# Expert block behind a router: token-major logits, positions ahead of the plan, scatter behind the second projection, last pass written out

## The reference, cut to what matters

```
h = h + concat(y_ssd, y_sc) @ w_out           # y_sc, y_ssd normed in groups
u2 = rmsnorm(h, norm_ffn)
p_group = softmax(u2 @ wg_r + bg_r); g_val, g_idx = top_k(p_group, 1)
sel = (u2 @ we_r + be_r) of the chosen group;  top_v, top_i = top_k(sel, 2)
combine = one_hot(g_idx) * g_val * softmax(top_v) at top_i
for e in 16 experts (4 groups of 4):
    out += combine[:, e] * ((silu(u2 @ w_gate[e]) * (u2 @ w_up[e])) @ w_down[e])
return rmsnorm(h + out, norm_final)
```

## Time and profile before

| | us |
|---|---|
| median of 3 runs (lowest, highest) | 1699.01 (1698.69, 1701.52) |
| the profiled execution's own time | 1698.8 |
| its span in the trace | 1697.0 |
| TensorE busy in the span | 1619.1 (95%) |
| end of the output projection, about | 1350.7 |
| first expert matmul | 1375.25 |
| last matmul of the last D3 ends | 1682.67 |

### The profile page before, as it was taken

One profiled execution on the slowest core, in us unless ns is written; L12 is line 12 of the kernel. 1 busy time (PEld: TensorE's weight loads), 2 busy tenths in 40 slices (PEclk: granted clock), 3 DMA queues, 4 the chain that ended last, 5 costly groups with the idle time before them and its releaser, 6 DMA issues.

```text
span 1697.0 us, 30496 instructions
## 1 busy us (share of the span) xinstructions
PE 1619.1 (95%) x11968; PEld 1502.0 (89%) x11968; DVE 1143.2 (67%) x1392; ACT 872.9 (51%) x1044; POOL 120.8 (7%) x89
## 2 busy tenths in 40 slices
PE   6999999989999999999998999999999879999996
PEld 6999978879999999997887999989999768778785
DVE  6655666656555655567666555578687479888887
ACT  5434434554433643443465443385535256767775
POOL 1000051010000100014001000021210000000000
PEclk9999999999999999999999999999999989999998
DMA  7766641145565566664013655646432759898993
GB/s 237 241 193 195 155 149 51 42 124 183 176 195 176 173 215 200 186 169 142 29 51 125 199 187 183 180 127 196 149 111 96 265 160 366 303 359 307 350 311 120
DMA packets 238218, 313.02 MB, mean 184 GB/s; under 512 B 51172, under 2 KB 176676, under 8 KB 238132
## 3 DMA queue, kind: packets, MB, share of 16 engines
q1 hardware_dynamic: 237520, 310.75, 56.6%
q10 hardware_dynamic: 612, 1.14, 0.2%
HBM read 310.82 MB, written 1.05 MB: 184 GB/s over the span
## 4 chain that ended last, share of the span: by engine, by line
issue 49%; PE 38%; DVE 3%; POOLq 3%; POOL 2%; ACT 2%; DVEq 1%; DMA 1%; SPq 0%; ACTq 0%
PE psum L416 6%; PE psum L418 6%; PE psum L417 6%; PE psum L2653 3%; PE psum L2652 3%; PE psum L2654 3%; PE psum L2675 2%; PE psum L2676 2%; PE psum L2677 2%; PE psum L2611 1%; POOL TMP L427 1%; POOLq L433 1%; POOLq L1518 1%; POOL QCOS L1533 1%; PE psum L2633 1%
## 5 line engine op out<-in xcount | busy, mean ns | idle before, releaser
L408 DVE TENSOR_TENSOR unit_low<-unit_raw,unit_high 128x2048 fp32r<-128x2048 f32 (+1 forms) x186 | 429.6, 2310 | 224.2 <-ACT unit_high L402 224.1
L416 PE MATMUL psum<-UH,unit_high 128*128 128x256 f32 x1888 | 541.8, 287 | 17.1 <-DVE UL L466 13.8
L417 PE MATMUL psum<-UL,unit_high 128*128 128x256 f32 x1888 | 534.8, 283 | 0.0
L418 PE MATMUL psum<-UH,unit_low 128*128 128x256 f32 x1888 | 534.5, 283 | 0.0
L402 ACT ACTIVATE unit_high<-unit_raw 128x2048 fp32r<-128x2048 f32 (+1 forms) x186 | 347.8, 1871 | 120.2 <-PE psum L418 119.7
L416 PEld LDWEIGHTS psum<-UH,unit_high 128*128 128x128 f32 x1888 | 361.1, 191 | 22.6 <-DVE UL L466 16.1
L417 PEld LDWEIGHTS psum<-UL,unit_high 128*128 128x128 f32 x1888 | 360.0, 191 | 1.6 <-issue 1.4
L418 PEld LDWEIGHTS psum<-UH,unit_low 128*128 128x128 f32 x1888 | 361.3, 191 | 0.0
L2395 DVE TENSOR_TENSOR unit_low<-unit_raw,unit_high 128x2048 fp32r<-128x2048 f32 x99 | 222.3, 2286 | 29.3 <-ACT unit_high L2391 29.3
L2391 ACT ACTIVATE unit_high<-unit_raw 128x2048 fp32r<-128x2048 f32 x99 | 184.7, 1917 | 14.8 <-PE psum L2677 8.7
L417 PE MATMUL psum<-HL,unit_high 128*128 128x256 f32 x640 | 178.9, 280 | 0.0
(11 more groups left out here) (490 smaller groups left out, 2503.1 us busy)
## 6 DMA issues: line engine op xcount, KB each, us to landing
unit_raw<-in_ffn_wg SPq DMA_DIRECT2D x44, 1024.0 KB
unit_raw<-in_ffn_wu SPq DMA_DIRECT2D x44, 1024.0 KB
unit_raw<-in_ffn_wd SPq DMA_DIRECT2D x44, 1024.0 KB
unit_raw<-in_w_in SPq DMA_DIRECT2D x36, 1024.0 KB
unit_raw<-in_expert_w_gate SPq DMA_DIRECT2D x34, 1024.0 KB, 7.4
unit_raw<-in_expert_w_up SPq DMA_DIRECT2D x33, 1024.0 KB, 7.8
unit_raw<-in_expert_w_down SPq DMA_DIRECT2D x32, 1024.0 KB, 7.3
unit_raw<-in_w_out SPq DMA_DIRECT2D x10, 1024.0 KB
```

What stands on the lines that cost most here:

```text
L408: dve.tensor_tensor(low[s][:, 0:w], raw[s][:, 0:w], high[s][:, 0:w].bitcast(F32), ALU.subtract).then_inc(unit_low, 1)
L416: pe.matmul(dst, wh, xh, start=start, stop=False, skip_group_check=True)
L417: pe.matmul(dst, wh, xl, start=False, stop=False, skip_group_check=True)
L418: return pe.matmul(dst, wl, xh, start=False, stop=stop, skip_group_check=True)
```

## The change

Two edits lie in the hybrid part. TensorE's `states(1)` waits for `yd1`, one VectorE instruction earlier than `yt1`. The short norm's last piece gets a tile of its own (`H`), its deviation is made before the SSD branch's, and its norm and split stand ahead of units 3 and 4 on VectorE. The logits are made with X held still, two products of 20 columns for each k, directly token-major, and half of the transposes and logits stand inside the projection's last unit, before its last two output tiles.

In the router, ScalarE and VectorE take expert unit 0 ahead of the logits, one of four squares goes to VectorE as `tensor_tensor_reduce`, half of `UTF` goes to GpSimd, positions and `select` stand ahead of the plan. Five units are split ahead instead of three. In a pass the scatter stands behind U0, T3 ahead of the gather; a projection waits for that half of `UL` which it reads. The last pass is written out behind the loop: no gather, no units ahead, T3 between the two units of D2, h's last split in `UH` and `UL`. The split of y, the scatter and the tail's sums and outputs go by halves of 512 columns.

The core of the diff (8 columns of indentation are taken off):

```diff
         elif h == 15:
-            pe.wait_ge(EM.sem, EM.at("yt1"))
+            pe.wait_ge(EM.sem, EM.at("yd1"))
...
+        for n in range(2):
+            mm = pe.matmul(psum[:, 0, n * 20:n * 20 + 20], X[:, k, META + n * P:META + n * P + P], WRG[:, k, :],
+                           start=(k == 0 and n == 0), stop=(k == KT - 1), skip_group_check=True)
         if k == KT - 1:
...
             if u == 7 and d % 2 and d < KT - 1:
                 mm.then_inc(QM.sem, QM.inc(f"out{d // 2}"))
+            if u == 7 and d == 5:
+                for n in range(4):
+                    to_tokens(n)
...
-    for k in range(KT):
-        to_tokens(k)
+    for n in range(4, KT):
+        to_tokens(n)
...
+def short_dev(j):
+    return (H if j == 3 else SG)[:, :, 0:T]
...
+        if kind == 2 and j in (1, 2):
             short_high(j - 1)
+    short_std(3)
     y_std(2)
+    short_high(2)
     w_high(act, 3)
-    short_std(3)
     w_high(act, 4)
     short_high(3)
...
         dve.wait_ge(BM.sem, BM.at(f"sc_std{j}"))
-        dve.reciprocal(SG[:, :, 0:T], SG[:, :, 0:T])
...
     def short_low(j):
...
             for gq in range(4):
                 pair_weights(2, gq)
-        elif i == 11:
-            short_low(2)
     normed_outputs(2)
+    short_low(2)
+    short_norm(3)
     w_low(dve, 3)
-    short_norm(3)
+    short_low(3)
     w_low(dve, 4)
-    short_low(3)
     w_low(dve, 5)
...
     w_low(dve, 7)
+    expert_low(dve, G2, 0)
...
-AHEAD = 3
+AHEAD = 5
...
+def last_h(j, more):
+    return (hh4, hl4) if more or j < 3 else (UH[:, 0:4, 0:P], UL[:, 0:4, 0:P])
...
-    pe.wait_ge(BM.sem, BM.at("xt1"))
-    gather_pe(pe, 0)
+    pe.wait_ge(EM.sem, EM.at("position"))
...
 def router_act(act):
+    expert_high(act, 0, G2, 0, used(G2, EU - 2))
     act.wait_ge(QM.sem, QM.at("x_t0"))
     for n in range(2):
         ins = act.activation(XTK[:, n, 0:512], psum[:, 4 + 2 * n, :], ACT.Copy)
     ins.then_inc(BM.sem, BM.inc("xt0"))
     for n in range(2):
         act.activation((sg_flat, h_flat)[n], psum[:, 4 + 2 * n, :], ACT.Square, accum_out=SS[:, n, 0:1])
-    expert_high(act, 0, G2, 0, used(G2, EU - 2))
+    expert_high(act, 0, G2, 1, used(G2, EU - 1))
...
+       .then_inc(BM.sem, BM.inc("ss"))
     act.wait_ge(EM.sem, EM.at("ss_sum"))
     act.activation(RS[:, 2:4], RS[:, 0:2], ACT.Sqrt, scale=1.0 / D, bias=eps[:, :]).then_inc(BM.sem, BM.inc("u_std"))
-    for n in range(2):
-        ins = act.activation(XTK[:, n, 512:D], psum[:, 5 + 2 * n, :], ACT.Copy)
-    ins.then_inc(BM.sem, BM.inc("xt1"))
-    expert_high(act, 0, G2, 1, used(G2, EU - 1))
+    act.activation(XTK[:, 0, 512:D], psum[:, 5, :], ACT.Copy).then_inc(BM.sem, BM.inc("xt1"))
     act.wait_ge(EM.sem, EM.at("g_sub"))
...
+    expert_high(act, 0, G2, 2)
     evacuate_act(act, 0)
-    expert_high(act, 0, G2, 2)
+    expert_high(act, 0, G2, 3)
+    expert_high(act, 0, G2, 4)
     act.wait_ge(EM.sem, EM.at("t_sub"))
     act.activation(RT[:, :, 84:85], RT[:, :, 84:85], ACT.Exp).then_inc(BM.sem, BM.inc("t_exp"))
...
+    dve.tensor_copy(XTK[:, 1, 512:D], psum[:, 7, :])
+    dve.drain()
+    dve.tensor_tensor_reduce(out=hl4.rearrange("p m s -> p (m s)"), in0=XTK[:, 1, 512:D], in1=XTK[:, 1, 512:D], scale=1.0, scalar=0.0,
+                             op0=ALU.mult, op1=ALU.add, accum_out=SS[:, 1, 1:2])
+    dve.drain()
     dve.wait_ge(BM.sem, BM.at("ss"))
     dve.tensor_tensor(RS[:, 0:2], SS[:, :, 0], SS[:, :, 1], ALU.add).then_inc(EM.sem, EM.inc("ss_sum"))
     dve.drain()
     dve.wait_ge(BM.sem, BM.at("u_std"))
     dve.reciprocal(RS[:, 0:2], RS[:, 2:4])
...
-    dve.wait_ge(BM.sem, BM.at("xt1"))
-    for n in range(2):
-        dve.tensor_tensor(UTF[:, n, 512:D], XTK[:, n, 512:D], GAINF[:, 512:D], ALU.mult)
+    four = "p n (g e) -> p n g e"
+    dve.tensor_tensor(c(40, 56).rearrange(four, g=4), c(4, 20).rearrange(four, g=4),
+                      c(32, 36).unsqueeze(3).to_broadcast([P, 2, 4, 4]), ALU.mult)
+    dve.drain()
+    dve.tensor_reduce(c(102), c(108, 112), AX, ALU.add)
+    dve.tensor_reduce(c(56, 60), c(40, 56).rearrange("p n (g e) -> p n e g", g=4), AX, ALU.add)
+    dve.drain()
+    dve.tensor_scalar(c(103), c(102), -1.0, float((GROUPS - 1) * P), ALU.mult, ALU.add)
     dve.wait_ge(QM.sem, QM.at("counts"))
     dve.tensor_tensor(c(104, 108), psum[:, 2, 0:8].rearrange("p (n f) -> p n f", n=2), c(32, 36), ALU.mult)
+    dve.drain()
+    dve.tensor_reduce(c(100), c(104, 108), AX, ALU.add)
+    dve.drain()
+    dve.scalar_tensor_tensor(out=c(101), in0=c(100), scalar=float(P), in1=c(103), op0=ALU.is_gt, op1=ALU.mult)
+    dve.scalar_tensor_tensor(out=c(104), in0=c(100), scalar=-1.0, in1=c(102), op0=ALU.add, op1=ALU.add)
+    dve.drain()
+    dve.tensor_tensor(POSQ[:, :], RT[:, :, 101], RT[:, :, 104], ALU.add)
+    dve.tensor_tensor(POS0[:, :], RT[:, :, 101], RT[:, :, 104], ALU.add).then_inc(EM.sem, EM.inc("position"))
+    select(dve)
...
-    select(dve)
     expert_low(dve, G2, 1)
-    evacuate_dve(dve, 0)
+    evacuate_dve(dve, 0, lambda: expert_low(dve, G2, 2))
+    expert_low(dve, G2, 3)
...
-    dve.tensor_copy(POSB[:, :], psum[:, 3, 0:T]).then_inc(y_low, 1)
+    dve.tensor_copy(POSB[:, :], psum[:, 3, 0:T]).then_inc(y_low, 2)
+    expert_low(dve, G2, 4)
+def router_pool(pool):
+    pool.wait_ge(gains_in, 32)
+    pool.wait_ge(BM.sem, BM.at("xt1"))
+    for n in range(2):
+        ins = pool.tensor_tensor(UTF[:, n, 512:D], XTK[:, n, 512:D], GAINF[:, 512:D], ALU.mult)
+    ins.then_inc(HM.sem, HM.inc("utf"))
...
     pe.wait_ge(selected, q + 1)
     for half in range(2):
+        if half and isinstance(q, int):
+            pe.wait_ge(HM.sem, HM.at("utf"))
...
+    for half in range(2):
+        pe.wait_ge(y_low, 2 * q + (half + 1))
+        for n in range(2):
+            for part, y in enumerate((YTH, YTL)):
                 mm = pe.matmul(psum[:, SCATTER_B[n] + half, :], SELT[:, n * P:n * P + P], y[:, half * 512:half * 512 + 512],
                                start=(part == 0), stop=(part == 1), skip_group_check=True)
-        mm.then_inc(scattered, 1)
+            mm.then_inc(scattered, 1)
 def add_dve(dve, q, n):
-    dve.wait_ge(scattered, 2 * q + (n + 1))
...
+    def down(g, j, q, more):
         pe.wait_ge(h_low, (4 * q + (EB + j)) + 1)
+        hh, hl = last_h(j, more)
         for u in range(2):
+            if j == 2 and u == 1 and not more:
+                transposes(3, q)
...
+                if j == 3 and u == 1 and half == 0:
+                    mm.then_inc(y_half, 1)
...
-    with pe.Fori(0, passes) as q:
+    def one_pass(q, more):
         g = G2 + 8 * q
...
-        projection(G_B, g, 0, 0)
+        projection(G_B, g, 0, 0, q)
+        projection(U_B, g, 0, 1, q)
         pe.wait_ge(EM.sem, EM.at("comb"))
         for n in range(2):
             mm = pe.matmul(psum[:, W_B, 0:4], SEL[:, n, :], RT[:, n, 92:96], start=(n == 0), stop=(n == 1))
         mm.then_inc(w_gathered, 1)
         scatter_pe(pe, q)
-        projection(U_B, g, 0, 1)
         for j in range(1, PER_GROUP):
             pe.wait_ge(silu, 4 * q + (EB + j))
-            projection(G_B, g, j, 0)
+            projection(G_B, g, j, 0, q)
             transposes(j - 1, q)
-            projection(U_B, g, j, 1)
+            projection(U_B, g, j, 1, q)
             if j == 1:
                 pe.wait_ge(added, 2 * q + 2)
-            down(g, j - 1, q)
-        gather_pe(pe, q + 1)
-        transposes(3, q)
-        down(g, 3, q)
-    pe.wait_ge(ug_low, 2 * passes + 2)
-    scatter_pe(pe, passes)
+            down(g, j - 1, q, more)
+        if more:
+            transposes(3, q)
+            gather_pe(pe, q + 1)
+        down(g, 3, q, more)
+    with pe.Fori(0, last) as q:
+        one_pass(q, True)
+    one_pass(last, False)
+    scatter_pe(pe, last + 1)
 def expert_act(act):
...
-        expert_high(act, q, g, 3)
+        act.activation(STD[:, 0:1], eps[:, :], ACT.Silu)
...
+        high_step(3, q, more)
+        if more:
+            evacuate_act(act, q + 1)
+            for d in range(3):
+                expert_high(act, q, g, PASS_UNITS + d)
+        act.wait_ge(y_half, q + 1)
+        act.activation(YTH[:, 0:512], psum[:, Y_B, :], ACT.Copy).then_inc(y_high, 1)
         act.wait_ge(unit_used, used(g, EU + unit_of(3, 2, 1)))
-        act.activation(halves(YTH[:, :]), psum[:, Y_B:Y_B + 2, :], ACT.Copy).then_inc(y_high, 1)
+        act.activation(YTH[:, 512:D], psum[:, Y_B + 1, :], ACT.Copy).then_inc(y_high, 1)
+        if more:
+            for d in range(3, AHEAD):
+                expert_high(act, q, g, PASS_UNITS + d)
+    with act.Fori(0, last) as q:
+        one_pass(q, True)
+    one_pass(last, False)
+    act.activation(STD[:, 0:1], eps[:, :], ACT.Sqrt, bias=eps[:, :])
...
         g = G2 + 8 * q
-        expert_low(dve, g, 3)
+        expert_low(dve, g, 5)
         dve.wait_ge(w_gathered, q + 1)
         dve.tensor_copy(WSLOT[:, :], psum[:, W_B, 0:4])
+        dve.drain()
+        product(g, 0, q)
         for n in range(2):
```

(47 more changed lines are left out.)

147 lines of the change are left out of this document (63 added, 84 removed), and 4 rows, old and new, of the table EM.

## The result

The changed kernel takes 1669.62 us, the median of 4 runs (1666.82 to 1675.16), the one before 1699.11 (1698.69 to 1701.52) beside it: a ratio of 0.9828 with a 95% interval of 0.9816 to 0.9841. The forecast was 1674.6 in 1669.5 to 1681. So the time lies 5 us under the forecast and only 0.1 us inside the range's lower end; that it lies inside is luck, with executions that spread over 8 us. The nine executions of the changed kernel in this study (four here, five in the first experiment) have a median of 1671.6, and 27 of the kernel before one of 1699.4: a gain of 27.8 where 24.4 was forecast.

What follows compares the result with a forecast made beforehand. TensorE, busy 95% of the span, was taken to bound the kernel. The terms summed to 24.4 us off the profiled 1698.8, giving 1674.4, or 1674.6 as a median; the range was 1669.5 to 1681.

Steps and rivals of the forecast that it cites:

- first projection: First projection behind the router's gather: needs only the ready first half of `UL`; 1.1 us gained, bounds 0.5 and 1.5.
- `yd1`: Hybrid part, TensorE's `states(1)`: waiting one VectorE addition less gains 1.1 us, bounds 0 and 1.3.
- Last short norm: Output projection: the 4.97 us wait for the last `YL` goes and the clock stays up; 7.0 us gained, bounds 4.5 and 7.3.
- The rival in which the wait only moves: Output projection: `YL` or SSD split 3 us later than counted, clock falls again, 5 us lost: 1679.5; chance 0.10.
- Tokens and logits: Projection's last unit: a stall of 0.7 to 0.9 us against cheaper logits pieces; net 0.3 us gained.
- From logits to the chain: Router, logits to VectorE's chain: about 2.6 us instead of 3.2, reduction taken as 1.0; 0.6 us gained.
- `UTF` and positions: Router chain: 1.3 us of VectorE work removed, 2.1 lost to blocking by GpSimd's products; net -0.8 us.
- The rival without blocking: Router: GpSimd's products and the tiny VectorE operations don't meet; 2.1 us less, 1672.5; chance 0.17.
- Scatter behind U0: Passes: U0 covers the 1.3 us wait for `comb`, but unit 6 is some 1.2 late in the first pass; 0.2 gained.
- T3 ahead of the gather: Three pass boundaries: D2's end to D3 shortens by 1.9 us each; 5.7 us gained, bounds 5 and 5.8.
- the rival of VectorE as the bound: Each pass's start: VectorE lacks 1 to 2 us before units 6 and 7; 6 us come back, 1680.5; chance 0.13.
- Tail: From D3's last start to the span's end: 10.5 us instead of 14.3; 3.8 us gained, bounds 2.5 and 4.5.

Runs made afterwards that it cites:

- the first experiment: The changed kernel run again with no edit: 1672.21 us (1667.92 to 1672.61), ratio 0.9825 to the kernel before.
- the second profile of before: The kernel before the change, run once more without edit to get another profile: 1699.18 us.
- `yt1`'s: The changed kernel with TensorE's wait at the 15th half unit on `yt1` again instead of `yd1`: 1670.29 us, ratio 0.9822.
- `UTF` on VectorE: The changed kernel with the second half of `UTF` on VectorE behind the selection instead of on GpSimd: 1671.30 us, ratio 0.9826.
- all together: The changed kernel with first pass written out without scatter and sums, MT before the taps, `UTF` on VectorE, fillers of 18 and 4 matmuls: 1665.81 us, ratio 0.9805.

## Why the prediction was right, and where it was not

The mechanisms came as forecast; two sizes and one reason did not. The term most off is the first projection's, and with it the clock in the gather.

*`yd1`, 1.1 forecast, 0.87 measured.* The size was near, the reason not: "TensorE is busy from there on, so I take 1.1". It is busy up to MT only, where it stood 0.48 in the profile before and stands 0.91 now. The 0.87 is what VectorE's chain to MT gained, 37.28 us from `yd1` instead of 38.14; had that chain not hung on `states(1)`, the gain would have been nothing.

*Last short norm, 7.0 forecast, 7.75 measured* (8.15 of the segment less 0.4 for the logits): wait and mechanism as said; the clock's share was 3.4 instead of 2.4 (low for 6.8 us, not 5.2), the wait's 4.4. The rival in which the wait only moves fell: the last `YL` came at 1317.9 in the profile, 3.2 later than counted, 2.9 of it by the fall of the clock at 1293, and TensorE, late by the same, did not wait.

*Tokens and logits, 0.3 forecast,* 0.4 measured, with the stall of 0.8: what is left of 66.70 against 64.62 with the short norm as it was, less 1.7 of the clock.

*From logits to the chain, 0.6 forecast.* From the last product's end (1357.73 before, 1352.80 after) to the chain's start (1360.95, 1355.18) it took 3.22 and now 2.38: 0.84. The unknown reduction takes 0.69 and not 1.0.

*`UTF` and positions, -0.8 forecast.* Chain start to the second half of SEL: 5.89 before (ends 1366.84), 6.40 now (1361.58): -0.5. The blocking is 1.75 instead of 2.1, shown by the kernel without it. The rival without blocking is out.

*First projection, 1.1 forecast, 3.26 measured* (8.02 to 4.76). Mis-sized: "The gather itself still runs at the lower clock, since TensorE idles as long before it: 0". It runs so for 2.5 us only and takes 4.76 instead of 6.50, 1.74 that the sum put at nothing; the wait for `UL` and what stood with it gave 1.52 where 1.1 was forecast. Both profiles of before have the long gather, eight of the changed form a shorter way from gather to G0 (4.5 to 6.0, a gain of 2.1 to 3.5). That the position matmuls ahead of it are the reason is not shown: no kernel moved them alone.

*Scatter behind U0, 0.2, and T3 ahead of the gather, 5.7 forecast.* (The prediction's own terms, 5.82 less 4.05, give 1.77 a boundary and not 1.9; 1.90 was measured.) Passes 0 to 2 together give 1.69, 1.92 and 1.88, 5.5 instead of 5.9. T3's part was measured by itself at 5.7; unit 6 is late by 1.5 instead of 1.2. That no later pass has a wait for it is as said; the rival of VectorE as the bound holds in pass 0 alone.

*Last pass, 5.4 forecast,* 5.48 measured. *Tail, 3.8 forecast,* 4.1: from D3's last start to the end 10.6 us. Both are read from segments, which repeat to a tenth in every profile of a changed kernel; no kernel undid either of them alone. The 4.1 is against the first profile of before, it would be 5.0 against the second.

The sum of the parts is 0.87 + 7.75 + 0.4 + 0.84 - 0.5 + 3.26 + 5.5 + 5.5 + 4.1 = 27.7; the profiled execution shows 23.6, as it loses 3.3 by the clock behind MT and 0.86 ahead of `yd1`. The medians give 27.8; that they agree so well is in part chance, as each execution has other falls of the clock. So the 24.4 was short by 3.3 in the parts: 2.2 by the first projection and 0.75 by the short norm, the clock's share in both above all.

## What to carry to other kernels

A wait that an edit shortens is worth only as much as the next wait behind it lets through: follow the waiting engine on to its next wait, however small (0.5 us here), and see whether the chain that ends there gets earlier too (0.87 of 1.3 us here). And measure the gain from an event that the edit doesn't move: from `states(1)` on it looked like nothing. Equal times of one event in two profiles prove nothing where the executions differ ahead of it (0.86 us here). Where one engine's total work up to a point is late, its order matters little: moving the sums moved most of the wait by one unit (0.5 gained), leaving them out, with their matmuls, gave 2.1 us. And where the spread of one kernel's times goes with the granted clock, compare segments between common events in the profiles; most repeat to 0.2 us where the times of one kernel spread over 8.

## What the runs showed of the hardware

- The clock's falls are not a fixed function of the program. Behind the same wait of 0.9 us for MT it fell to the lower level (1.2 GHz) once in eight profiles, behind the wait of 0.78 at `to_tokens` twice in eleven, behind that of 1.9 ahead of `states(1)` in two of three (the second profile of before and `yt1`'s), behind that of 1.34 for `comb` in one of two, and once each behind 1.96 (`UTF` on VectorE) and 1.6 us (all together). Behind the 1.65 at the pass ends it never fell, in eleven such waits. The Trainium skill ("TensorE: Matmul & The Clock Gate", Why this matters for your kernels) names gaps over about 3 us as those to avoid; in these profiles shorter ones, of 0.78 to 1.96 us, were followed by a fall in some executions as well. That the wait is the cause of such a fall is not shown, since the clock also falls in stretches that no edit touches.
- Some low stretches stand in every profile of both kernels at the same place (near 365 and 915 us, 1.7 to 3.4 us of loss each), others come and go (near 15, 290, 560 and 840). With the idle time of the router filled with matmuls (two kernels) the clock stayed up in it, in all eleven other profiles it was low there.
- `tensor_tensor_reduce` of 512 columns with its accumulator: 0.69 + 0.08 us, as a plain product of 512 columns (0.69).
- GpSimd's 512-column products held up VectorE's operations with two inputs in SBUF, 8 columns wide, until each ended (0.94 and 1.15 instead of 0.17). The reduction with one input that ran 0.1 us behind the first product's start took its usual 0.16.
